# The attention stage of a hybrid decoder layer: heads and key tiles issued one by one in another order

## What is computed

```python
score = where(causal, sum_h(relu(q_idx @ k_idx.T) * w_idx), -inf)
_, sel = top_k(score, 128)                       # the keys each query may see
s = (q_lat @ kv_sel.T) * 64 ** -0.5              # 8 heads, one shared latent
p = softmax(where(sel <= qpos, s, -inf))
o_lat = p @ kv_sel                               # then w_uv per head, then w_out
y_ml = sigmoid(o_m) * layer_norm(h_mlstm)        # the other half, 4 heads
out = concat([y_att, y_ml]) @ w_out
```

## Time and profile before

| | |
|---|---|
| median of three executions | 1017.39 us |
| profiled execution | 1017.49 us |
| its span in the trace | 1015.8 us |
| PE busy in the span | 996.9 us (98%) |
| DVE busy | 714.0 us (70%) |
| ACT busy | 493.8 us (49%) |
| POOL busy | 118.1 us (12%) |
| attention, rounds 0 to 8 | 529.5 to 600.1 us of the span |

### The profile page before, as it was taken

One profiled execution on the slowest core, in us unless ns is written; L12 is line 12 of the kernel. 1 busy time (PEld: TensorE's weight loads), 2 busy tenths in 40 slices (PEclk: granted clock), 3 DMA queues, 4 the chain that ended last, 5 costly groups with the idle time before them and its releaser, 6 DMA issues.

```text
span 1015.8 us, 18999 instructions
## 1 busy us (share of the span) xinstructions
PE 996.9 (98%) x7028; PEld 907.9 (89%) x7028; DVE 714.0 (70%) x1317; ACT 493.8 (49%) x868; POOL 118.1 (12%) x92
## 2 busy tenths in 40 slices
PE   9999999999999999999999999999999999999996
PEld 8999999999999988699765668889999999988886
DVE  6988888887322264699997523699989889942236
ACT  6656665566121264546346522576656665812121
POOL 0000000001121262045302205320000000000000
PEclk9999999999999999999999999999999999999999
DMA  7233332323223313132110102113323232333212
GB/s 252 84 100 107 102 105 90 116 80 105 86 86 111 113 44 116 36 123 82 44 42 1 43 1 83 43 42 126 124 83 124 85 121 96 125 103 101 98 57 84
DMA packets 30849, 90.48 MB, mean 89 GB/s; under 512 B 4689, under 2 KB 5329, under 8 KB 30801
## 3 DMA queue, kind: packets, MB, share of 16 engines
q1 hardware_dynamic: 30800, 89.83, 26.7%
HBM read 87.72 MB, written 2.10 MB: 88 GB/s over the span
## 4 chain that ended last, share of the span: by engine, by line
PE 81%; DVE 15%; ACT 2%; issue 1%; DMA 0%; SPq 0%; DVEq 0%; ACTq 0%
PE ps L1229 38%; PE ps L1287 22%; PE ps L1152 9%; DVE sc L2201 3%; DVE top L2200 3%; PE ps L1714 2%; PE ps L1424 1%; PE ps L1692 1%; DVE qk L2240 1%; PE ps L1705 1%; DVE wlo L1877 1%; PE ps L1489 1%; PE ps L1722 1%; PE ps L1337 1%; PE ps L1335 1%
## 5 line engine op out<-in xcount | busy, mean ns | idle before, releaser
L1229 PE MATMUL ps<-tsum,whi 128*128 128x264 f32 (+1 forms) x1280 | 243.1, 282 | 0.5 <-ACT ht L790 0.5
L1229 PEld LDWEIGHTS ps<-tsum,whi 128*128 128x128 f32 x1280 | 202.3, 188 | 0.7 <-issue 0.7
L1229 PE MATMUL ps<-tsum,wlo 128*128 128x264 f32 (+1 forms) x640 | 180.3, 282 | 0.0
L1229 PE MATMUL ps<-xh,whi 128*128 128x264 f32 (+1 forms) x480 | 135.4, 282 | 0.3 <-ACT sil L790 0.3
L1229 PE MATMUL ps<-xl,whi 128*128 128x264 f32 (+1 forms) x480 | 135.5, 282 | 0.0
L1229 PE MATMUL ps<-xh,wlo 128*128 128x264 f32 (+1 forms) x480 | 135.3, 282 | 0.0
L729 ACT ACTIVATE whi<-wraw 128x1408 fp32r<-128x1408 f32 (+1 forms) x48 | 74.6, 1555 | 123.0 <-PE ps L1287 123.0
L1787 DVE TENSOR_TENSOR wlo<-wraw,whi 128x1408 fp32r<-128x1408 f32 (+1 forms) x38 | 70.0, 1843 | 85.3 <-ACT whi L729 85.3
L1287 PE MATMUL ps<-hh,whi 128*128 128x264 f32 (+1 forms) x462 | 124.2, 323 | 0.0
L1287 PE MATMUL ps<-hh,wlo 128*128 128x264 f32 (+1 forms) x462 | 123.5, 322 | 0.0
L1287 PE MATMUL ps<-hl,whi 128*128 128x264 f32 (+1 forms) x462 | 123.4, 321 | 0.0
(11 more groups left out here) (287 smaller groups left out, 1828.0 us busy)
## 6 DMA issues: line engine op xcount, KB each, us to landing
wraw<-in_ffn_w_gate SPq DMA_DIRECT2D x43, 512.0 KB, 4.2
wraw<-in_ffn_w_up SPq DMA_DIRECT2D x42, 512.0 KB, 4.3
wraw<-in_ffn_w_down SPq DMA_DIRECT2D x32, 384.0 KB, 3.2
wraw<-in_ffn_w_down SPq DMA_DIRECT2D x32, 320.0 KB, 3.5
wraw<-in_w_in SPq DMA_DIRECT2D x19, 512.0 KB, 4.5
wraw<-in_w_out SPq DMA_DIRECT2D x8, 512.0 KB, 4.4
out<-zrow SPq DMA_DIRECT2D x8, 256.0 KB, 2.0
x<-in_x SPq DMA_DIRECT2D x3, 528.0 KB, 7.5
```

Source lines behind the costliest of these rows:

```text
L1229: mm = pe.matmul(ps[:, bank, 0:(HT, HALF_SEQ)[p // 2]], w[:, k * P:(k + 1) * P], v[:, k, :], start=(first and k == 0 and n == 0), stop=(k ...
```

## The change

In each round the two halves (heads q0 and q1, heads q2 and q3) give way to single steps. On PE, the order of a round was: two scores; project; turns of tiles 0 and 1; two scores; then weighs and the remaining turns. It becomes: two scores; project; turns 0 and 1; score q2; weigh 0; turn 2; score q3; weigh 1; turn 3; and so on. On DVE and ACT the copies of tile 2 and of tiles 3 and 4 move between and behind the single heads in the same manner, and `normalise` moves behind the mask of q2. The mLSTM products of DVE and ACT and the late rounds of `select` all move to the end of their round. Head by head, `gated_mlstm` stood in rounds 1, 1, 2, 3, and stands in the same ones, but at their end; `normed_mlstm` of head 3 stays in round 2, but at its end; `mlstm_hi` stood in rounds 1, 2, 3, 4, and stands at the end of rounds 2, 2, 3, 4. No instruction is added or taken away, no shape or type is changed.

```diff
-HEAD_GATED = ((1, 0), (1, 1), (2, 1), (3, 1))
-HEAD_HI = ((1, 1), (2, 0), (3, 0), (4, 0))
+HEAD_GATED = (1, 1, 2, 3)
+HEAD_HI = (2, 2, 3, 4)
-LATE_AT = ((4, 0), (4, 1), (5, 0))
+LATE_AT = (4, 4, 5)
@@ ACT, attention
-                    for half in range(2):
-                        if G < GROUPS:
-                            exps(G, (2 * half, 2 * half + 1))
-                        if half == 0:
-                            if G >= 1:
-                                copy_odd(G - 1, (0, 1))
-                        if (G, half) in HEAD_HI:
-                            mlstm_hi(HEAD_HI.index((G, half)))
+                    if G < GROUPS:
+                        exps(G, (0, 1))
+                    if G >= 1:
+                        copy_odd(G - 1, (0, 1))
+                    if G < GROUPS:
+                        exps(G, (2,))
+                    if G >= 1 and last_tile >= 2:
+                        copy_odd(G - 1, (2,))
+                    if G < GROUPS:
+                        exps(G, (3,))
                     if G >= 1:
-                        copy_odd(G - 1, range(2, j + 1))
+                        copy_odd(G - 1, range(3, j + 1))
                         act.wait_ge(pv_step, TP0[G])
...
                         act.activation(olt[g], ps[:, 3, :], ACT.Copy).then_inc(ol_ready, 1)
+                        for h in range(ML_H):
+                            if HEAD_HI[h] == G:
+                                mlstm_hi(h)
@@ PE, attention
-                    for half in range(2):
-                        if G < GROUPS:
-                            for q in (2 * half, 2 * half + 1):
-                                scores(4 * G + q)
...
+                    if G < GROUPS:
+                        scores(4 * G)
+                        scores(4 * G + 1)
+                    if G == 0:
+                        turn_mlstm((0, 1))
+                    if late is not None:
+                        project(late)
                     if G >= 1:
-                        for i in range(last_tile + 1):
-                            if 2 <= i + 1 <= last_tile:
-                                turn(G - 1, i + 1)
+                        turn(G - 1, 0)
+                        turn(G - 1, 1)
+                    if G < GROUPS:
+                        scores(4 * G + 2)
+                    if G >= 1:
+                        weigh(G - 1, 0)
+                        if last_tile >= 2:
+                            turn(G - 1, 2)
+                    if G < GROUPS:
+                        scores(4 * G + 3)
+                    if G >= 1:
+                        for i in range(1, last_tile + 1):
                             weigh(G - 1, i)
+                            if i + 2 <= last_tile:
+                                turn(G - 1, i + 2)
@@ DVE, attention
+                    if G < GROUPS:
+                        masked(4 * G)
+                        masked(4 * G + 1)
                     if G >= 1:
-                        copy_even(G - 1, range(2, last_tile + 1))
+                        copy_even(G - 1, (0, 1))
+                    if G < GROUPS:
+                        masked(4 * G + 2)
+                    if late is not None:
+                        normalise(late)
+                    if G >= 1 and last_tile >= 2:
+                        copy_even(G - 1, (2,))
+                    if G < GROUPS:
+                        masked(4 * G + 3)
+                    if G >= 1:
+                        copy_even(G - 1, range(3, last_tile + 1))
+                    if G in (0, 2):
+                        normed_mlstm((2 + G // 2,))
+                    for h in range(ML_H):
+                        if HEAD_GATED[h] == G:
+                            gated_mlstm((h,))
+                    late_rounds(G)
+                    if G >= 1:
                         if late is not None:
                             att_lo(late)
```

More of the change, by code:

```diff
@@ L1098, in attention @@
                 for G in range(GROUPS + 1):
-                    for half in range(2):
-                        if G < GROUPS:
-                            exps(G, (2 * half, 2 * half + 1))
-                        if half == 0:
-                            if G >= 1:
-                                copy_odd(G - 1, (0, 1))
-                        if (G, half) in HEAD_HI:
-                            mlstm_hi(HEAD_HI.index((G, half)))
+                    last_tile = 1 + (G - 1) // 2
+                    if G < GROUPS:
[8 more added lines that the diff above has]
+                        exps(G, (3,))
                     if G >= 1:
                         j, g = 1 + (G - 1) // 2, (G - 1) % 2
-                        copy_odd(G - 1, range(2, j + 1))
+                        copy_odd(G - 1, range(3, j + 1))
                         act.wait_ge(pv_step, TP0[G])
@@ L2370, in copy_even, with late_rounds @@
                             dve.tensor_copy(pt_flat[0:ROWS[i], 0:512], ps[0:ROWS[i], 0, :]).then_inc(pt_even, 1)
[L2372 to L2375, removed]
+                def late_rounds(G):
+                    for n, at in enumerate(LATE_AT):
+                        if at == G:
+                            select(4, LATE_ROUND + n, LATE_ROUND + n + 1)
@@ L2377, in attention @@
                 for G in range(GROUPS + 1):
                     last_tile = 1 + (G - 1) // 2
[L2379 to L2392, removed]
```

1 line of the change is left out of this document (removed).

## The result

The changed kernel takes 1022.71 us (median of 7 executions, 1019.9 to 1023.93); the kernel before took 1017.03 us beside it (7 executions, 1016.82 to 1017.8). The ratio is 1.005, with a 95% interval of 1.0037 to 1.0063: 0.5% slower, and outside the range of 1017.6 to 1021.0. The profiled execution took 1022.6 us, 5.1 more than that of before, with a span of 1020.9 us.

The account below looks back on a forecast made before the run. PE, busy 98% of the span, was taken as the bound, so only its waits or work count. Terms +0.72 + 1.17 - 0.6 + 0.55 = +1.8 us on 1017.39 gave 1019.2 us; range 1017.6 to 1021.0.

Parts of the forecast that it names:

- the step on the clock: Attention stage: more PE idle than the two new stretches of 0.5 to 1.0 us had kept clock 1.00, so no fall.
- the clock rule: PE pausing often between matmul groups as it changes PSUM banks can make the clock swing; 1029 us, chance 0.02.
- Round 1, +0.72: Head 0's gated product, now behind the mask of q3, makes PE's transposition of head 2 wait: 0.72 us later.
- Round 2, +1.17: PE waits 1.0 us for head 3's normalisations, now behind both masks, and 0.3 for score q2; +1.17 us in the sum.
- Rounds 3 to 5, -0.6: Waits for copies of tile 2 go and selection rounds leave PE's path: 0.24 + 0.1 + 0.3, about -0.6 us.
- Round 6, +0.55: Weigh of tile 3 waits for ACT's copy, behind the exponential of later score q3; +0.55 us in the sum.
- round 7, nothing: One more turn and weigh between score q3 and the weigh needing ACT's copy cover it by 0.1 us: no loss.
- The sum of the waits: All attention rounds together: +0.72 + 1.17 - 0.6 + 0.55 = +1.8 us, moving the kernel's end by as much.
- Rival 4: The clock rule: 10 us of PE work at the lower level of 1.2 GHz, 1029 us; chance 0.02.
- Rival 1: Rounds 5, 6 and 7: late exponentials delay ACT's copy of the fourth tile; slower, 1020.5 us; chance 0.20.
- Rivals 2, 3 and 5: New order covers more than it loses, 1018.3 us, 0.13; PE's idle goes, 1014.6 us, 0.06; nothing moves, 1017.4 us, 0.03.

Follow-up runs that it names:

- the experiment: Changed kernel with idle PE products ahead of weigh 0, 3 in round 1 and 4 in round 4: 1020.03 us, ratio 1.0022 to the kernel before.

## Why the prediction was wrong

- **What failed is the step on the clock.** It said that the trace before "does not bear it out", because 2.77 us of idle time in 73 had been granted 1.00, and gave the clock rule 0.02. The sum of idle time was the wrong measure, since it does not say where the idle time lies. Score q3 used to lie in the gap ahead of weigh 0 and went out of it. The gap grew from 0.26 to 0.60 us in round 1 and from 0.48 to 1.22 in round 4, and the clock fell there. The prediction worked out the start of weigh 0 in both rounds, found it unmoved or 0.28 later, and did not write down that PE has less to do ahead of it; the new idle time that it weighed against the clock was in rounds 1 and 2 alone, and no fall came behind the 0.90 us wait of round 2. Filling the gap of round 4 took the slow executions away (four of five without, none of ten with the products). What the gap does not explain is why three other traces with one as long kept the whole clock. The Trainium skill ("TensorE: Matmul & The Clock Gate", section "A second HAM failure mode: psum-queue depth-cycling") had the rule that PE pausing often between groups of matmuls lets the clock swing; the trace after agrees, at 0.50 in two stretches, and the traces of the same gap at 1.00 say that it need not. My price for it was also wrong: I had 10 us of work at the lower level, where two stretches of 3.4 us cost 2.4 us in the traces (2.6 with the 0.2 of the experiment's own edit), and 2.8 to 3.3 by the timing.
- **Round 1, +0.72.** Right in mechanism, measured 0.93 at a whole clock. The missing 0.2 is small lags, in the trace at a whole clock: the mask starts 0.55 us after score q3 and not 0.49, PE starts 0.13 after the end of head 0's product and not 0.03, and the scores of round 2 follow the transpositions 0.47 later, not 0.44. (The chain of waits puts the transpositions at 0.63 instead of 0.44, since it counts to a modelled end.)
- **Round 2, +1.17.** Right, 1.39 (1.33 in the changed kernel itself), missing 0.2 in the same way. The releaser is DVE's `upad`, as forecast. At a whole clock the transpositions start at 545.04, 2.3 us later than 542.70, where 1.9 was forecast; in the changed kernel's own trace, which has the first fall ahead of it, they start at 546.25.
- **Rounds 3 to 5, -0.6.** Measured -0.46 with a whole clock (-0.18, -0.03, -0.25). The two selection rounds at the end of round 4 cost nothing, covered by the projection, as forecast.
- **Round 6, +0.55, and round 7, nothing.** Measured 0.70 and 0.07 (0.63 and 0.00 in the changed kernel itself).
- **The sum of the waits**, 1.8, is 2.63 in the trace without a fall and 2.4 by the timing with products. The prediction would have been 0.6 us off with it alone (2.4 against 1.8), and inside its range: 1020.0 us lies in 1017.6 to 1021.0. So the waits were forecast, and the clock was not.
- **The rivals.** Rival 4, with 0.02, named the cause and had its size three to four times too large. Rival 1 is not borne out: late exponentials cost 0.6 to 0.7 us in round 6 and nothing in rounds 5 and 7. Rivals 2, 3 and 5 fall with the waits of rounds 1, 2 and 6, which the traces show. The spread of the executions, 4 us against 1 us before, goes with the clock: of the seven, the two at 1019.9 and 1020.0 have a mean clock of 0.997, the five at 1022.6 to 1023.9 have 0.994. What part of the highest ones is left when two falls are taken off is open, as is why a fall comes in one execution and not in the next.

## What to carry to other kernels

When work is moved out of a place where PE waits, its cover is gone even if nothing starts later: write down the idle gap of each wait before and after, not only the time of the release, and treat a grown gap as a possible fall of the clock. A few idle products in such a gap, shorter than the gap, are a cheap test of that, and can be the cure. One trace does not settle it: the same kernel fell in some executions and not in others, so look at the spread of the times and at the mean clock of each execution. An order that is interleaved on several engines is to be judged round by round: here it gained 0.5 us in three rounds and lost 3 in three others, and keeping it in the three that gain, with the mLSTM work at its old places, took 0.6% off the changed kernel and 0.1%, just clear of the noise, off the one before.

## What the runs showed of the hardware

- A clock at half level for 3.4 us cost 1.0 us in round 1, where PE would have waited anyway (7.18 against 6.19 us), and 1.6 in round 4, where it had work (12.09 against 10.51).
- What PE did ahead of the second fall: it waited 0.25 us for score q2, worked 0.94, waited 1.22, and was 1.0 us into weigh 0 and what follows. In the 5 us up to there it was busy 3.54 us. In the trace with the mLSTM waits removed, which kept the whole clock, it was busy 3.53 us up to the same place, and in that with products in round 1 alone 3.44. So busy time of this kind did not decide it alone.
- Four float32 transpositions count as 0.44 us in the chain of waits in a running stream, and as 0.63 to 0.66 behind a wait. From their start to that of the next product the timeline shows 0.44 and 0.47 to 0.50 us, so most of the difference is in the view.
